# An RWKV scan in residual form: both heads' state held as one 128-column block-diagonal matrix

## The reference, cut to what matters

```python
def step(s, inp):
    w_t, a_t, k_t, v_t, kk_t = inp[:5]
    s = (s * w_t[:, :, None, :]
         - jnp.einsum('bhvk,bhk->bhv', s, kk_t)[..., None] * (kk_t * a_t)[:, :, None, :]
         + v_t[..., None] * k_t[:, :, None, :])
    y = jnp.einsum('bhvk,bhk->bhv', s, inp[5]) if emit else None
    return s, y
```

## Time and profile before

| | |
|---|---|
| median of 3 runs | 4084.01 us (4083.36 to 4095.02) |
| span of the profiled execution | 4085.5 us |
| the four scans | 854 to 941, 998 to 1086, 2964 to 3050 and 3110 to 3196 us |
| TensorE / VectorE / ScalarE / GpSimd busy over the span | 90% / 55% / 26% / 12% |
| mean granted TensorE clock | 0.945 of full speed |

### The profile page before, as it was taken

How to read it: one execution, slowest core, us unless ns; L and a number is a source line. 1 busy time by engine, 2 the same in 40 slices (tenths; PEclk the granted TensorE clock), 3 DMA queues, 4 the chain that set the end, 5 groups by cost and what they waited for, 6 DMA issues and landing times. The chain is left out here.

```text
span 4085.5 us, 66177 instructions
## 1 busy us (share of the span) xinstructions
PE 3690.0 (90%) x27408; PEld 2046.7 (50%) x27408; DVE 2226.9 (55%) x3700; ACT 1064.1 (26%) x2366; POOL 491.0 (12%) x675
## 2 busy tenths in 40 slices
PE   7899999687896899999998899997697968999998
PEld 4555665476643333333334655664586533333333
DVE  3554324688756544444443554335778667655654
ACT  3442110634311111111112542113444211111121
POOL 1100000221210111111111200000232110010100
PEclk9899999688998999999999899998798989999999
DMA  7200120200276577788873000211100336999996
GB/s 264 94 1 11 60 75 0 90 3 19 70 296 234 182 267 267 268 273 273 269 254 99 32 1 11 73 56 58 33 10 13 120 133 245 336 326 335 319 332 200
DMA packets 293592, 613.14 MB, mean 150 GB/s; under 512 B 37640, under 2 KB 50184, under 8 KB 286640
## 3 DMA queue, kind: packets, MB, share of 16 engines
q1 hardware_dynamic: 272752, 542.32, 37.2%
q0 software_dynamic: 20544, 66.60, 6.3%
HBM read 561.07 MB, written 47.79 MB: 149 GB/s over the span
## 5 line engine op out<-in xcount | busy, mean ns | idle before, releaser
L3017 PE MATMUL ps<-moe_w,e_hT 128*128 128x512 f32 x1024 | 449.4, 596 | 21.5 <-issue 8.9
L3148 DVE TENSOR_TENSOR moe_w<-moe_w 128x2048 f32<-128x2048 f32 x128 | 287.2, 2286 | 200.5 <-PE ps L2947 157.2
L2917 PE MATMUL ps<-moe_w,e_xs 128*64 128x512 f32 x1536 | 348.6, 596 | 0.8 <-DVE moe_w L3148 0.8
L2917 PE MATMUL ps<-moe_w,e_xT 128*64 128x512 f32 x1536 | 340.6, 592 | 0.8 <-DVE moe_w L3148 0.8
L3017 PEld LDWEIGHTS ps<-moe_w,e_hT 128*128 128x128 f32 x1024 | 192.3, 190 | 258.4 <-issue 255.6
L3154 DVE TENSOR_TENSOR e_cb<-e_part,ps 128x512 f32<-128x512 f32 x128 | 87.9, 686 | 335.1 <-ACT e_part L3056 249.3
L2917 PEld LDWEIGHTS ps<-moe_w,e_xT 128*64 128x64 f32 x1536 | 110.7, 137 | 218.7 <-issue 218.7
L2917 PEld LDWEIGHTS ps<-moe_w,e_xs 128*64 128x64 f32 x1536 | 105.3, 137 | 193.8 <-issue 192.3
L1197 PE MATMUL ps<-M 96*128 96x512 f32 (+1 forms) x400 | 183.2, 544 | 2.9 <-PEq L748 2.1
L3056 ACT COPY e_part<-ps 128x512 f32<-128x512 f32 x96 | 56.3, 586 | 480.7 <-PE ps L2917 472.4
L1057 PE MATMUL ps<-yT,hT 128*128 128x272 f32 (+1 forms) x608 | 148.1, 399 | 1.6 <-DMA yT<-in_w_in_dram 1.6
(11 more groups left out here) (420 smaller groups left out, 7163.9 us busy)
## 6 DMA issues: line engine op xcount, KB each, us to landing
moe_w<-in_w_gate_dram SPq DMA_DIRECT2D x128, 1024.0 KB, 14.1
moe_w<-in_w_up_dram SPq DMA_DIRECT2D x128, 1024.0 KB, 14.2
moe_w<-in_w_down_dram SPq DMA_DIRECT2D x128, 1024.0 KB, 13.2
m_mod_w<-in_w_ada_dram SPq DMA_DIRECT2D x24, 1024.0 KB, 6.6
o_mod_w<-in_w_ada_dram SPq DMA_DIRECT2D x24, 1024.0 KB, 7.6
yT<-in_w_in_dram SPq DMA_DIRECT2D x6, 2048.0 KB, 7.8
r_z<-z_rows SPq DMA_DIRECT2D x20, 512.0 KB, 3.3
z_rows<-p_zo POOLq DMA_DIRECT2D x36, 256.0 KB, 2.3
```

The source lines that it names most:

```text
L2917: ins = nc.tensor.matmul(ps[HF * q:HF * q + HF, b, :], x[:, k], weights[q][:, k], start=(first and k == 0), stop=(k == 3), skip_group_chec ...
L3017: ins = nc.tensor.matmul(ps[:, YB + c, :], hT2[:, 4 * half + k], quarter(name, e)[:, k], start=(half == 0 and k == 0), stop=(half == 1 and ...
L3148: nc.vector.tensor_tensor(to, a, b, ALU.subtract).then_inc(*td.up())
```

## The change: the residual form

The recurrence over a chunk is solved for the residual instead: R = (decayed removal keys) x S, then U = T x (M V - R), with M V the chunk's inner part. So W1 and W2 are gone, and with them w1_w2, w_out and the waits for them.

- S becomes a block-diagonal matrix of 128 x 128, one head in each diagonal block, with a buffer less. carry_r multiplies it in one product for both heads (K = 128 rows, 64 stationary columns, 128 streamed) and starts the output with a second one (128 stationary columns, 64 streamed).
- ScalarE copies R, negated, into the half of TS that is free for the chunk (r_out). carry_u is now four 64 x 64 x 64 products (T times MV and T times R for each head), which all read one half of the partitions and write the same half. ScalarE copies U into the values' token rows (u_out).
- carry_s is then one 128 x 128 x 128 product (keys and removal keys together against values and U together) and two of 128 x 64 x 64 for the output. VectorE writes S in two instructions, one for each head, with the decay folded in; L2050 and L2056 go.
- The values for the inner part are formed by inner (was m_v), early in the round, beside the inverse. The products of the next tile wait for the last level_t alone.
- TS and MV have two buffers. GpSimd fills the next tile's TS once the carry of the tile before last is over, and makes KE, the keys and queries times the decay of the chunk before (four more instructions in a round).
- In stage_rwkv_prep a unit of by_token becomes four products with 64 stationary columns against the identity and two transposes of the values, for both directions; the halves of the diagonal blocks change places, the decays ET are shifted by one chunk, and ScalarE copies 512 columns for each unit.
- The four parts of the masks stand in another order. BYTOK takes four slots for both directions.

The new lines and the loops, cut to the core (removed functions stand above, in the kernel before; m_v, w1_w2, w_out, mv_out and scale_of, decayed and VectorE's carry_u go):

```diff
-                for a, src in enumerate(sources(d)):
-                    ins = nc.tensor.transpose(ps[:, TBANKS[u % 4], a * P:(a + 1) * P], src[:, t * P:(t + 1) * P], g.ident)
+                b = TBANKS[u % 4]
+                for c in range(2):
+                    for a in range(2):
+                        r0, t0 = CH * (c if a else 1 - c), t * P + CH * c
+                        nc.tensor.matmul(ps[r0:r0 + CH, b, c * P:(c + 1) * P], BK[d][:, a, t0:t0 + CH], g.ident, start=True, stop=True)
+                for c in range(2):
+                    ins = nc.tensor.transpose(ps[:, b, (2 + c) * P:(3 + c) * P], M[:, 4 + p, t * P:(t + 1) * P], g.ident)
                 ins.then_inc(*turned.up())
...
-                        ins = nc.tensor.matmul(ps[32 * c:32 * c + 32, DBANKS[d][h], 32 * t:32 * t + 32],
+                        r0 = 32 * ((c + 2) % 4)
+                        ins = nc.tensor.matmul(ps[r0:r0 + 32, DBANKS[d][h], 32 * t:32 * t + 32],
...
+                def carry_r(d, s, q):
                     n, c = 2 * s + q, chunks[d][q]
                     if q == 0:
+                        pe.wait_ge(*kd[d].at(s + 1))
                         if n_y(d, s):
                             pe.wait_ge(*ye[d].at(n_y(d, s)))
+                    pe.wait_ge(*su[d].at(n + 1))
+                    Sn = S[d][:, n % 2]
+                    nc.tensor.matmul(ps[HALF[1 - c], CA[d], Rc], KE[d][:, s % 2, 0, HALF[c]], Sn, start=True, stop=True).then_inc(*rm[d].up())
+                    if has_y(d, s):
+                        nc.tensor.matmul(ps[:, YB[d], HALF[c]], Sn, KE[d][:, s % 2, 1, HALF[c]], start=True, stop=False,
+                                         skip_group_check=True)
+                def carry_u(d, s, q):
+                    n, c = 2 * s + q, chunks[d][q]
+                    if q == 0:
+                        pe.wait_ge(*ts[d].at((s + 1) * (NLV + 1)))
+                        pe.wait_ge(*me[d].at(s + 1))
+                    pe.wait_ge(*re[d].at(n + 1))
                     for h in range(2):
+                        out = ps[HALF[1 - c], CA[d], Uc.start + CH * h:Uc.start + CH * h + CH]
+                        for first, src in ((True, MV[d][HALF[1 - c], s % 2, h]), (False, TS[d][HALF[1 - c], s % 2, 0, h])):
+                            ins = nc.tensor.matmul(out, TS[d][HALF[1 - c], s % 2, 1, h], src, start=first, stop=not first)
+                    ins.then_inc(*umm[d].up())
+                def carry_s(d, s, q):
+                    n, c = 2 * s + q, chunks[d][q]
+                    pe.wait_ge(*ue[d].at(n + 1))
+                    nc.tensor.matmul(ps[:, CA[d], Pc], key_rows(d, s, c), value_rows(d, s, c), start=True, stop=True).then_inc(*smm[d].up())
                     if has_y(d, s):
                         for h in range(2):
+                            ins = nc.tensor.matmul(ps[HALF[h], YB[d], HALF[c]], value_rows(d, s, c)[:, HALF[h]], UM[d][:, s % 2, h, 2 + c],
+                                                   start=False, stop=True, skip_group_check=True)
+                        if q == 1:
+                            ins.then_inc(*ym[d].up())
+                def inner(d, s):
+                    pe.wait_ge(*um[d].at(s + 1))
+                    for h in range(2):
+                        for c in range(2):
+                            ins = nc.tensor.matmul(ps[HALF[1 - c], LV[d] + 1, MVc.start + CH * h:MVc.start + CH * h + CH],
+                                                   UM[d][HALF[c], s % 2, h, 1], value_rows(d, s, c)[HALF[c], HALF[h]], start=True, stop=True)
+                    ins.then_inc(*mm[d].up())
...
+                                half = HALF[c if a else 1 - c]
+                                out = ps[half, LV[d] + h, 0:4 * CH].rearrange("p (b n) -> p b n", n=CH)[:, a:3 + c:2 + c - a]
+                                ins = nc.tensor.matmul(out, BK[d][HALF[h], a, toks(d, s, c)], KR[d][HALF[h], :, toks(d, s, c)], start=True, stop=True)
                     ins.then_inc(*p1[d].up())
...
                 for s in range(NT + 1):
                     inv, car = s < NT, s > 0
-                    for d in DD:
-                        if car:
-                            w1_w2(d, s - 1)
                     for d in DD:
                         if inv:
                             products(d, s)
                         if car:
+                            carry_r(d, s - 1, 0)
+                    for d in DD:
+                        if car:
                             carry_u(d, s - 1, 0)
                     for d in DD:
                         if inv:
-                            m_v(d, s)
+                            inner(d, s)
+                            level_x(d, s, 0)
+                    for d in DD:
                         if car:
                             carry_s(d, s - 1, 0)
-                        if inv:
-                            level_x(d, s, 0)
                     for d in DD:
+                        if car:
+                            carry_r(d, s - 1, 1)
                         if inv:
                             level_t(d, s, 0)
+                    for d in DD:
                         if car:
                             carry_u(d, s - 1, 1)
-                    if inv:
-                        level_x(0, s, 1)
-                    if car:
-                        carry_s(0, s - 1, 1)
-                    if inv:
-                        level_x(1, s, 1)
-                        level_t(0, s, 1)
-                    if car:
-                        carry_s(1, s - 1, 1)
-                    if inv:
-                        level_t(1, s, 1)
+                        if inv:
+                            level_x(d, s, 1)
+                    for d in DD:
+                        if car:
+                            carry_s(d, s - 1, 1)
+                        if inv:
+                            level_t(d, s, 1)
...
                 def carry_s(d, s, q):
                     n, c = 2 * s + q, chunks[d][q]
+                    k = 2 * order[d][s] + c
                     dve.wait_ge(*smm[d].at(n + 1))
-                    nc.vector.scalar_tensor_tensor(S[d][:, (n + 1) % 3], ps[:, CA[d] + c, Sc], scale_of(d, s, q), Se[d][:],
-                                                   ALU.mult, ALU.add).then_inc(*su[d].up())
+                    for h in range(2):
+                        ins = nc.vector.scalar_tensor_tensor(S[d][HALF[h], (n + 1) % 2, HALF[h]], S[d][HALF[h], n % 2, HALF[h]],
+                                                             ET[d][HALF[h], 1, k:k + 1], ps[HALF[h], CA[d], 2 * P + CH * h:2 * P + CH * h + CH],
+                                                             ALU.mult, ALU.add)
+                    ins.then_inc(*su[d].up())
...
-                        if s:
-                            pool.wait_ge(*wm[d].at(s))
+                        if s >= 2:
+                            pool.wait_ge(*umm[d].at(2 * (s - 1)))
...
+                    for d in DD:
+                        t = order[d][s]
+                        if s >= 2:
+                            pool.wait_ge(*rm[d].at(2 * (s - 1)))
+                        for a in range(2):
+                            ins = nc.gpsimd.tensor_tensor(KE[d][:, s % 2, a].rearrange("p (c n) -> p c n", c=2),
+                                                          KR[d][:, a, t * P:(t + 1) * P].rearrange("p (c n) -> p c n", c=2),
+                                                          ET[d][:, 1, 2 * t:2 * t + 2].unsqueeze(2).broadcast_to([P, 2, CH]), ALU.mult)
+                        ins.then_inc(*kd[d].up())
...
+                def r_out(d, s, q):
+                    n, c = 2 * s + q, chunks[d][q]
+                    act.wait_ge(*rm[d].at(n + 1))
+                    nc.scalar.activation(TS[d][HALF[1 - c], s % 2, 0], ps[HALF[1 - c], CA[d], Rc].rearrange("p (u n) -> p u n", u=2), ACT.Copy, scale=-1.0).then_inc(*re[d].up())
+
+                def u_out(d, s, q):
+                    n, c = 2 * s + q, chunks[d][q]
+                    act.wait_ge(*umm[d].at(n + 1))
+                    nc.scalar.copy(value_rows(d, s, c)[HALF[1 - c]], ps[HALF[1 - c], CA[d], Uc]).then_inc(*ue[d].up())
...
+                def inner_out(d, s):
+                    act.wait_ge(*mm[d].at(s + 1))
+                    nc.scalar.activation(MV[d][:, s % 2].rearrange("p u n -> p (u n)"), ps[:, LV[d] + 1, MVc], ACT.Copy, scale=-1.0).then_inc(*me[d].up())
```

More of the change, by code:

```diff
@@ L103, in constants @@
     after, from_ = i[:, None] % CH > j[None, :], i[:, None] % CH >= j[None, :]
-    masks = np.stack([np.stack([strict, incl, strict, incl], 1), np.stack([after, from_, after, from_], 1)], 1).astype(f)
+    masks = np.stack([np.stack([strict, strict, incl, incl], 1), np.stack([after, after, from_, from_], 1)], 1).astype(f)
     nlev = np.zeros((P, 2, len(TOP), CH), f)
@@ L1794, in _ @@
                 nc.scalar.activation(BK[d][:, 0], G[d][:], ACT.Exp, scale=-LWC).then_inc(*exd.up())
```

(39 more changed lines are left out.)

125 lines of the change are left out of this document (43 added, 82 removed).

## The result

The changed kernel takes 4265.4 us (median of 4 runs, 4261.9 to 4270.1), the kernel before 4085.9 beside it; the ratio is 1.043, 95% interval 1.0415 to 1.0452. It is slower, as forecast, but by 179 us where 95 were forecast, and it lies above the range.

The account below looks back on a forecast made before the run. TensorE was taken to bound the scan round (8.15 to 9.9 us) and the prep inversion: scans +57 and inversion +38 make +95 us on 4085.5, so 4180, or 4179 at the median; range 4092 to 4228.

Parts of the forecast that it names:

- TensorE sets the round: Scan: TensorE has the least room, so its work sets the round, 9.9 us instead of 8.15; chance 0.71.
- The chain sets the round: Rival, scan: wide records overlap like small ones, round 6.73 us, kernel 4055, faster; chance 0.09.
- the change of shape is free: Rival, scan and prep inversion: alternating tile shapes falls into waits, round 7.8 us, kernel 4093; chance 0.12.
- The changes of shape: Scan, TensorE: 21 alternations of tile shape a round at 0.10 us each, 2.1 us.
- The ring: Prep stage inversion: each by_token unit 0.86 us instead of 0.385; 26 us instead of 16.5, 38 in four passes.
- The issue sum: Scan, TensorE: record times of all products in a round, without shape alternation, 7.53 us against 6.9 before.
- W stretch: Old scan round: w1_w2 and the wait for W copies, a pure chain of 1.42 us that the change removes.
- changes at 0.05: Lower price for each tile shape alternation, giving the low end of the forecast's own range, 4125 us.
- The wait for y_out: Scan: next round's first carry_r, queued behind VectorE's output write, comes 0.3 us late each round.
- First and last round: Scan ends: first as before, last only carry, 5.6 + 0.7 us against 6.4 before; cost nothing.
- The saving by rounds without output: Second layer: two rounds of each pass lack output, some 3 us less a pass, 6 in all.
- with 0.15 a change: Rival, dearer shape alternation: round 11.0 us, scans +97, prep inversion +46, 4227; chance of over 4228: 0.08.

Follow-up runs that it names:

- e_alt: Changed kernel with by_token's value transposes in the prep stage spread between the BK products, same instructions; 4290.0 us, ratio 1.0475 to the kernel before.
- e_quad: Changed kernel with U's products of the two directions issued turn by turn instead of one direction after the other; 4243.6 us, ratio 1.0362 to the kernel before.
- e_resid_q: Kernel before with residual form and T doubled, all products 64x64x64, U's products of both directions turn by turn; 4118.7 us, ratio 1.0063.

## Why the prediction was wrong in size

**TensorE sets the round: right.** Busy 78.7 of 80.1 us. "The chain sets the round" (4055) and "the change of shape is free" (4093) both fell; nothing was faster.

**The changes of shape: the step that failed.** The prediction took 0.10 us a change, at most 0.15. Read the changed kernel's round from 903.02 to 914.46 record by record. At each of the 21 changes the first record of the new shape starts about 0.09 to 0.11 late. The second one is another 0.05 late, and 0.10 in the four state products. That is 0.14 us a change and 0.20 at the state products, 3.2 us in all. The ring gives 0.15, with e_alt as its direct test. The error was in how were read. I measured the interval from the last record of one shape to the first of the next, 0.20 instead of 0.10, and took the difference. But the second record is late too, and that lies behind the interval. The rows held it: in the earlier trace rows the two records that start at 211.44 reach to 211.81, 0.37 us for 2 x 0.11. The term was 2.1 us and measured 3.2.

**The issue sum: low by 0.4.** In the same round R and the state product keep their 0.11 a record between changes, as taken. The output starts (L1939) were priced at 0.098. But in the earlier trace rows the eight records from 782.53 to 783.42, of which four are of this shape, take 0.11 each: the four looked shorter because the delay falls behind them. This is 0.12 of the 0.42. The level_t products took 1.39 instead of 1.30. For U the rate in one quarter, 0.053 a record by proportion, measured 0.058. Its first group with the inner products was forecast at 1.55 and took 1.22 net of changes, the second at 0.85 and took 1.34. That the two directions would share the time in the second was wrong: they follow each other, and only e_quad's order makes them share it.

**Two slips in the prediction's own sums.** The old round was said to be 6.9 us of issue and 1.42 of W stretch. But W's 32 records are in both; counted once, 7.5 of the 8.15 are explained. And with changes at 0.05 the terms give 4134, not 4125. Neither moves the forecast.

**The wait for y_out: right**, 0.20 where 0.3 was forecast.

**First and last round: forecast at nothing.** Right for the first, which takes 6.4 us from its products to the next ones (before 7.8, the W stretch among them). The last, which only carries, was forecast at 6.3 us. TensorE's first R of it and VectorE's last S:

```profile
974.49 0.40 PE L1937 MATMUL ps<-s_S,s_KE 128*64 128x128 f32 x2 [0.63 <-issue]
...
981.16 1.26 DVE L2046 SCALAR_TENSOR_TENSOR s_S<-s_S,rw_ET,ps 64x64 f32<-64x64 f32 x4 [2.44 <-PE ps L1959]
```

It takes 7.9, with 16 changes of shape, and the wait for y_out ahead of it is longer. That is 6 us in four passes. The saving by rounds without output was forecast at 6 us in all; the third pass is 4 us shorter than the first, the fourth 0.6, since it lost 3.5 to the clock.

**The ring: right in mechanism, the same term too small.** Forecast 26.0 us, measured 28.0. 20 units with two changes at 0.15 instead of 0.10 are the 2.0 us, and the prediction had this as its bound.

**The sum.** 57 + 38 = 95 forecast. A round of 1.54 us more over 36 rounds is 55, of which the changes make 1.1 a round and the issue sum 0.4. The last rounds add 6, the clock in the fourth pass 3.5, the ring 8: 168, against 177 in the spans. The remaining 9 or so lie in pieces that I didn't follow. So the price of a change is the largest miss, some 48 us with the ring, but not the only one: with 0.15 a change the prediction's own sum was 4227.

The Trainium skill (TensorEngine Tiling (Array Packing), Tiling Modes, Key Properties) says that a change of the tiling mode drains TensorE. The runs agree in that every change costs time, 0.14 to 0.20 us. Whether the array drains, no trace here shows.

Open stays what a residual round would be with both limits lowered at once, and what exactly TensorE does in the 0.15 us: the runs show its size and its two parts, no more. Nor do they show why the second part is twice as long in the state product.

## What to carry to other kernels

Price a change of shape by the length of a whole group after it, not by the one interval at its edge, and multiply it by the number of changes: in this loop, with groups of two to four records, it cost about as much as the records (four outputs 0.11 us, their change 0.14). Before merging small products into a wide one, write out the sequence of shapes; two products that keep their neighbours' shape were cheaper here than one that doesn't. And products that all fell into one quarter of the array passed at half the rate, unless another direction's were issued in turn with them. Where TensorE then waited for both directions' copies, the gain was lost again (e_resid_q).

## What the runs showed of the hardware

A change between 64 x 64, 128 x 64 and 128 x 128 products cost 0.14 to 0.15 us at full clock, in either direction: some 0.10 ahead of the first record and 0.05 between the first and the second. At the state product of 128 x 128 x 128 the second part was 0.10 and the whole 0.20; at the ring's transposes, of the same shape, the whole was 0.15. Two products of 128 x 64 x 64 with alternating column halves passed at 0.03 us a record (four in 0.12, and in 0.16 right behind a change), the one of 128 x 128 x 128 that they replace at 0.11 a record when its shape stays, and at 0.21 right behind a change. Records in one quarter followed each other every 0.058 us, in two quarters turn by turn every 0.029.
